# A weight unit of the input projection moved from one step of the attention loop to a later place, in a one-core decoder layer kernel

## What is computed

```python
h = x * (1 + sc1) + sh1
qa, ka, va, qb, kb, vb, ga, gb = jnp.split(h @ w_in, W_IN_SPLITS, axis=-1)
...
oa, ob, new_state = mixer(qa, ka, va, qb, kb, vb, pos)      # branch A dilated windows, branch B blocks
merged = (jax.nn.sigmoid(ga) * (oa.reshape(B, S, DSA_OUT) @ w_pa)
          + jax.nn.sigmoid(gb) * (ob.reshape(B, S, MOBA_WIDTH) @ w_pb))
x = _layer_norm(ALPHA * x + g1 * (merged @ w_o), ln1_g, ln1_b)
h2 = x * (1 + sc2) + sh2
up, gt = jnp.split(h2 @ w_up, 2, axis=-1)
x = _layer_norm(ALPHA * x + g2 * ((jax.nn.silu(gt) * up) @ w_down), ln2_g, ln2_b)
```

## Time and profile before

| quantity | value |
|---|---|
| median of 3 runs | 517.5 us (516.73 to 517.93) |
| the profiled execution, its own time | 516.83 us |
| its span in the trace | 515.3 us |
| TensorE busy | 504.5 us of the span |
| VectorE, ScalarE, GpSimd busy | 291.9, 223.8, 89.2 us |
| granted TensorE clock, mean | 0.998 of full |

### The profile page before, as it was taken

How to read it: one execution, slowest core, us unless ns; L and a number is a source line. 1 busy time by engine, 2 the same in 40 slices (tenths; PEclk the granted TensorE clock), 3 DMA queues, 4 the chain that set the end, 5 groups by cost and what they waited for, 6 DMA issues and landing times.

```text
span 515.3 us, 10082 instructions
## 1 busy us (share of the span) xinstructions
PE 504.5 (98%) x3954; PEld 461.3 (90%) x3954; DVE 291.9 (57%) x568; ACT 223.8 (43%) x372; POOL 89.2 (17%) x132
## 2 busy tenths in 40 slices
PE   7899999999999999999999999999999999999997
PEld 5578988888778998997998799999999999999996
DVE  0556776867445453446985875455555555366344
ACT  2334434325435644447435574654444444433312
POOL 2000212126621111000351428701001010000000
PEclk9999999999999999999999999999999999999999
DMA  8999998595988873855664736574757574354102
GB/s 275 392 395 392 381 391 296 170 375 178 307 290 281 273 268 120 233 182 183 222 190 162 245 94 189 172 273 161 268 174 258 168 259 173 124 179 164 42 1 92
DMA packets 85437, 115.80 MB, mean 225 GB/s; under 512 B 3785, under 2 KB 67465, under 8 KB 84884
## 3 DMA queue, kind: packets, MB, share of 16 engines
q1 hardware_dynamic: 83332, 102.59, 59.4%
q0 software_dynamic: 1824, 12.47, 6.6%
q10 hardware_dynamic: 240, 0.17, 0.1%
HBM read 111.94 MB, written 13.57 MB: 244 GB/s over the span
## 4 chain that ended last, share of the span: by engine, by line
PE 90%; DMA 4%; SPq 4%; DVE 1%; ACT 1%; issue 1%
PE psum L748 24%; PE psum L750 23%; PE psum L749 23%; DMA raw<-in_w_in 4%; PE psum L925 3%; PE psum L769 2%; PE psum L1045 2%; SPq L586 2%; PE psum L998 1%; PE psum L1031 1%; PE psum L989 1%; PE psum L1240 1%; PE psum L939 1%; PE psum L794 1%; PE psum L780 1%; PE psum L1116 1%
## 5 line engine op out<-in xcount | busy, mean ns | idle before, releaser
L500 DVE TENSOR_TENSOR w_lo<-raw,w_hi 128x1024 fp32r<-128x1024 f32 (+1 forms) x120 | 146.0, 1220 | 148.0 <-ACT w_hi L495 147.7
L748 PE MATMUL psum<-act_hi,w_hi 128*128 128x288 f32 x736 | 221.6, 301 | 0.2 <-DVE rope_t L1657 0.2
L749 PE MATMUL psum<-act_lo,w_hi 128*128 128x288 f32 x736 | 217.1, 295 | 0.0
L750 PE MATMUL psum<-act_hi,w_lo 128*128 128x288 f32 x736 | 216.5, 294 | 0.0
L495 ACT ACTIVATE w_hi<-raw 128x1024 fp32r<-128x1024 f32 (+1 forms) x120 | 124.1, 1041 | 101.9 <-PE psum L750 85.1
L748 PEld LDWEIGHTS psum<-act_hi,w_hi 128*128 128x128 f32 x736 | 138.0, 187 | 12.9 <-issue 11.2
L750 PEld LDWEIGHTS psum<-act_hi,w_lo 128*128 128x128 f32 x736 | 138.5, 188 | 0.0
L749 PEld LDWEIGHTS psum<-act_lo,w_hi 128*128 128x128 f32 x736 | 138.2, 188 | 0.1
L748 PE MATMUL psum<-f_hi,w_hi 128*128 128x288 f32 x176 | 52.3, 297 | 0.0
L749 PE MATMUL psum<-f_lo,w_hi 128*128 128x288 f32 x176 | 51.9, 295 | 0.0
L750 PE MATMUL psum<-f_hi,w_lo 128*128 128x288 f32 x176 | 51.8, 294 | 0.0
(11 more groups left out here) (222 smaller groups left out, 580.1 us busy)
## 6 DMA issues: line engine op xcount, KB each, us to landing
ada_s<-in_w_ada SPq DMA_DIRECT2D x22, 1024.0 KB, 11.1
raw<-in_w_up SPq DMA_DIRECT2D x22, 1024.0 KB, 5.1
raw<-in_w_in SPq DMA_DIRECT2D x17, 1024.0 KB, 9.9
raw<-in_w_down SPq DMA_DIRECT2D x10, 1024.0 KB, 5.0
out<-in_cache_kv_a POOLq DMA_DIRECT2D x16, 504.0 KB, 5.7
raw<-in_w_o SPq DMA_DIRECT2D x4, 1024.0 KB, 7.6
raw<-in_w_in SPq DMA_DIRECT2D x4, 768.0 KB, 11.2
kvin<-in_cache_kv_a SPq DMA_DIRECT2D x8, 256.0 KB, 3.6
```

The lines of the kernel that those rows point to most:

```text
L500: nc.vector.tensor_tensor(part(w_lo, slot4, by_rows), raw_half(rslot, hh, by_rows), part(w_hi, slot4, by_rows).bitcast(F32), ALU.subtract) ...
L748: nc.tensor.matmul(out, hi_l, hi_r, start=start, stop=False, skip_group_check=True)
L749: nc.tensor.matmul(out, hi_l, lo_r, start=False, stop=False, skip_group_check=True)
L750: return nc.tensor.matmul(out, lo_l, hi_r, start=False, stop=stop, skip_group_check=True)
```

## The change

Gate unit 15 leaves step 13 on TensorE and stands behind `outputs_turn(0)` in step 14, where the two unread matmuls were. Its copy on ScalarE and the split of half H_PAB + 3 on both engines move from step 13 to places behind the loop. ScalarE rounds branch A's outputs ahead of the first sigmoids, and two groups of sigmoids (22 to 24 and 28 to 32) stand ahead of the copy of gate unit 15. VectorE takes the rest of branch A's outputs in step 15 ahead of `out_copy(11)`, and splits H_PAB + 3 behind `oT_rest(1)`. The last group of sigmoids (14 to 18) waits for gate unit 15's copy. The results are the same.

```diff
@@ TensorE @@
         for s in range(1, 16):
-            if s + 2 < 16:
+            if s + 2 < 15:
                 gate(s + 2)
...
                 outputs_turn(0)
-                keep_warm(2)
+                gate(15)
@@ ScalarE @@
-            if s + 2 < 16:
+            if s + 2 < 15:
                 gate_copy(s + 2)
                 hi_static(act, H_GATE + s + 2 + AHEAD)
...
-        act.wait_ge(acc_free[0], 18)
-        act.wait_ge(acc_free[1], 18)
-        sigmoids(22, 24)
-
...
         oT_leading(0)
+        act.wait_ge(acc_free[0], 18)
+        act.wait_ge(acc_free[1], 17)
+        sigmoids(22, 24)
+        sigmoids(28, 32)
+        gate_copy(15)
         act.wait_ge(sel_done, 1)
         nc.scalar.activation(oT_hi[:, :, PROMPT:TOK], psum[:, 7, 0:4 * SAMPLE].rearrange("p (k c) -> p k c", c=SAMPLE),
                              ACT.Copy).then_inc(oT_h, 1)
-        sigmoids(28, 32)
         oT_leading(1)
+        hi_static(act, H_GATE + 15 + AHEAD)
         sigmoids(12, 14)
         sigmoids(24, 28)
+        act.wait_ge(acc_free[1], 18)
         sigmoids(14, 18)
@@ VectorE @@
-            if s + 2 < 16:
+            if s + 2 < 15:
                 lo_static(dve, H_GATE + s + 2 + AHEAD)
...
+            if s == 15:
+                oT_rest(0)
             if s >= 4:
                 out_copy(s - 4)
...
-        oT_rest(0)
         dve.wait_ge(oT_h, 2)
         V.tensor_tensor(oT_lo[:, :, PROMPT:TOK], psum[:, 7, 0:4 * SAMPLE].rearrange("p (k c) -> p k c", c=SAMPLE),
                         oT_hi[:, :, PROMPT:TOK].bitcast(F32), ALU.subtract).then_inc(oT_l, 1)
         oT_rest(1)
+        lo_static(dve, H_GATE + 15 + AHEAD)
```

## The result

The changed kernel takes 521.75 us (median of 4, 521.23 to 522.6) against 517.23 us before: a ratio of 1.0079, 95% interval 1.0058 to 1.0100, so some 4 us slower. The profiled execution took 521.95 us with a span of 520.4 us, 5.1 us more than before. In a later session (e12) the median was 521.1 us against 517.52 (ratio 1.0063, interval 1.0046 to 1.0080).

The account below looks back on a forecast made before the run. TensorE's work plus its waits was taken as the bound. A win of 1.24 us against waits of 1.92 and 0.6 us gave +1.3, the tail +0.2: +1.5 us, 519.0 us on the median, range 518.0 to 521.0.

Parts of the forecast that it names:

- The sign: Whole kernel: slower by more than the 1.03 us that can be told from no change, chance 0.77.
- The sum: Waits up to the branch projections +1.3 us and tail +0.2 us give +1.5 us, put on the median as 519.0 us.
- first rival: Clock falls in the uncovered wait of step 13, slowing the work behind: +1.7 us, 520.7 us, chance 0.17.
- The win, 1.24 us: Step 14, 236.13 to 237.37: the moved unit replaces unread matmuls and idle time, -1.24 us.
- First wait, 1.92 us: Step 13: without the unit, the last scores wait for VectorE's `maxed` until 228.95, 1.92 us.
- Second wait, 0.6 us: Transposes behind the last scores wait for ScalarE's `prbT_copy(9)` until 230.0, 0.6 us more.
- No third wait; 0.8 us ahead: Behind the two waits nothing else holds TensorE, which runs 0.8 us earlier than before up to branch A's turn.
- PAB later by 1.3 us: Start of the branch projections: -1.24 + 1.92 + 0.6 = +1.3 us, at 240.9 instead of 239.60.
- Tail, 0.2 us: Third quarter of PAB: ScalarE's chain grows from 3.95 to 4.17 us, TensorE waits +0.2 us, between 0 and 0.5.
- What costs nothing: Later load of `w_o`'s third chunk, later GpSimd cache rows, and table load and swapped rounding under the moved unit: no cost.
- The clock's chance: Fall of the clock in the new waits of step 13, 2.5 us of idleness within 3 us: chance 0.17.
- The clock's price: Half to all of the 48 sample matmuls at the lower level: 1.5 to 3 us, taken as 1.7 us.

Follow-up runs that it names:

- e12: The changed kernel itself, unaltered, measured again in a later session beside the kernel before: 521.1 us, ratio 1.0063.
- e1: The changed kernel with unread matmuls in both new waits, four ahead of the last scores and one ahead of the transposes: 518.86 us, ratio 1.0029.
- e5: The changed kernel with the split of H_PAB + 2 moved behind the softmax work of step 12 on ScalarE and VectorE: 516.97 us, ratio 0.9989.
- e10: e5 with ScalarE's split of the first half of `w_o` ahead of the last group of sigmoids: 516.19 us, ratio 0.9976.
- e4: The changed kernel with gate unit 15 cut: 18 matmuls in step 13, the last 6 behind branch A's turn: 519.48 us, ratio 1.0033.
- e6: The changed kernel with two unread matmuls in the first new wait and none in the second: 519.14 us, ratio 1.0036.
- e3: The changed kernel with gate unit 15 back in step 13 on TensorE and the unread matmuls back in step 14: 519.45 us, ratio 1.0044.
- e2: The kernel before without its two unread matmuls in step 14, nothing else: 518.53 us, ratio 1.0020.

## Why the prediction was right or wrong

The sign was right. The time was not: 519.0 us in a range of 518.0 to 521.0 was forecast, 521.75 was measured. The step that failed is the clock. The sum behind 519.0 let TensorE keep its pace behind the new waits; the fall of the clock stood beside it as the first rival, named with its place, given 0.17, and priced at 1.7 us. It is in both profiled executions of the changed kernel and cost 2.94 us in the first (PAB at 18.26 against 15.32 in e1) and 2.74 in the second (18.06), and the mean clock was low in all 15 executions. The likeliest case should have been that one, at 519.0 + 2.9 = 521.9 us. The range itself cut it off: the rival's own price went up to 3 us, that is to 522.0.

- **The win, 1.24 us.** Right: in the changed kernel the last values follow on the unit without a wait, and in e5, where little else is left, PAB comes 0.99 us earlier, close to 1.24 less the 0.24 us of the second wait.
- **First wait, 1.92 us.** Right in place and releaser (VectorE's `small`). The last scores start 3.57 us behind the first L998 row, and 228.95 - 225.30 = 3.65 was forecast. Its length came out a little shorter, 1.65 us idle and 1.72 us by starts (3.57 against 1.85 in e5, where they do not wait): TensorE follows VectorE's maximum after 0.06 us here (229.77 to 229.83) and not 0.14.
- **Second wait, 0.6 us.** Right: 0.61 us idle, 0.11 us behind the end of the copy that had been named (230.82 to 230.93). e5 shows the chain behind both, since moving one split removes the first and most of the second.
- **No third wait; 0.8 us ahead.** Right: in e1 branch A's turn starts at 9.52 against 10.38 before, 0.86 us earlier.
- **PAB later by 1.3 us.** A little too much: without the fall of the clock it is 15.32 - 14.30 = 1.02 us (e1). The unit's place behind the turn takes 3.64 us from the start of the turn to the last values (13.16 - 9.52), where 0.45 + 3.36 = 3.81 had been added up. In the changed kernel the turn takes 0.36 us up to the unit (238.73 to 239.09) and the unit 3.27 (239.09 to 242.36): the neighbours of a unit change its length from start to start by some 0.1 us. The last 0.07 us lie between the last values and PAB (2.16 us, 2.23 before).
- **Tail, 0.2 us.** Right: 6.71 against 6.52 us, and gone in e10.
- **What costs nothing.** Right behind 250: the third chunk of `w_o` is issued at 247.12, and from PAB's third quarter to the end the two kernels take the same time.
- **The sum.** With the waits filled it is 518.86 us against 517.52, that is +1.3 us, where +1.5 was forecast for waits and tail.
- **The clock's chance.** The argument for it was the fall "some 1.8 us" after the last matmul. Against it stood "there were other holes" ahead of that fall and "the work around 227 is denser". Both were misread. These are TensorE's last row with idle time in the kernel before and the stretch in which its clock fell at the end:

```profile
508.96 0.73 PE L1252 MATMUL psum<-gain_rows,stat_rows 6*128 6x512 f32 x4 [0.36 <-ACT stat_rows L1557]
```

```profile
513.50:514.00 0.50, 0.00 (x0) 0.00 (x0) 0.00 (x0) 0.00 (x0) 0.00 (x0) 0.63 0.87 320
```

A mean of 0.63 puts the fall near 513.6, that is 1.4 us behind the last matmul (512.22), and the only hole in the 10 us ahead of it is 0.36 us long. That was less idleness than the 2.5 us forecast for the new waits. And the stretch in which the clock then fell was not dense at all: TensorE was busy 1.35 of 3.00 us in 227 to 230 and 1.39 of 2.00 in 230 to 232.
- **The clock's price.** Too low: 1.7 us for 2.94. I took the sample matmuls alone, half to all of them. The values and transposes ahead of them ran at the lower level too (1.0 of the 2.95 us), and so did three quarters of the 48.

The Trainium skill (TensorE: Matmul & The Clock Gate, Part 1: The HAM clock gate) holds that throttling is the default and activity releases it. By that rule a wait that replaces dense work is a risk of its own; the trace agrees, with 0.50 in 232 to 236 behind 2.26 us of idleness in two pieces and 1.00 again from 238 on, when TensorE had been busy since 230.93. How sure the fall is behind such pieces, a low mean clock in 15 of 15 executions, is this case's measurement.

## What to carry to other kernels

A matmul unit in front of a wait is cover even when the profile shows no wait there: before moving it, subtract its length from the time that the next semaphore is early, and add what else is queued between. Then ask of each new wait of TensorE not only how long it is but what the clock will do with it, and price the clock by the work that runs behind, not by the wait: here 2.26 us of waiting brought 6.8 us at the lower level, which cost 2.94 us. If the cover must go, look on the waited-for engines for work that is early by far and stands ahead of the urgent one; moving one weight split turned +4 us into -0.7 us here (medians; -0.8 in the profiles from the first L998 row on), and with a second one into -1.3 us (-1.0 in the profiles).

## What the runs showed of the hardware

- The granted clock fell to 0.50 in the second of two idle pieces of 1.65 and 0.61 us, and in e12 already behind the first; it was back 6.8 us later in both, with TensorE busy nearly all the while. It fell likewise behind 0.29 and 1.53 us (e4), for 3.4 us, and stayed up in the profiled executions behind 0.73 and 0.61 us (e6), 0.21 and 1.52 us (e3) and 1.08 us (e2).
- At the lower level the sample matmuls took 0.63 us each and not 0.38, and the block of 48 took 4.94 us and not 3.00, though its last quarter ran at the upper level again.
- Without two matmuls whose result nobody reads, the median of the kernel before was 1.0 us higher, though they lie in a wait: 4 of 12 executions had a mean clock of 0.997 or less, with them none of 29 in the same session. In later sessions 1 of 35 and 6 of 34 executions of the kernel before had one too; where it fell in those is not known.
